# Dense matmuls of a two-block model on one core: operands at other word addresses within 256 words

## What is computed

```python
def hybrid_layer(x, ...):
    xn = rmsnorm(x, norm1_g)
    proj = xn @ w_in                       # split in eleven parts
    ...
    mixed = g_ssd * (y_ssd @ w_ssd_out) + g_mla * (y_mla @ w_mla_out) + g_gdn * (y_gdn @ w_gdn_out)
    h = x + mixed @ w_out
    f = jnp.square(jax.nn.relu(rmsnorm(h, norm2_g) @ w_up)) @ w_down
    return h + f

def swiglu(h, w_in, w_out):                # second model, widths 1024 -> 2 x 2816 -> 1024
    a, u = jnp.split(h @ w_in, 2, axis=-1)
    return (jax.nn.silu(a) * u) @ w_out
```

## Time and profile before

| | us |
|---|---|
| median of 3 runs (2468.61 to 2469.38) | 2469.3 |
| the profiled execution, whole | 2476.37 |
| its span (first to last instruction) | 2474.5 |
| TensorE busy | 2375.8 (96%) |
| weight loads busy | 2197.9 (89%) |
| VectorE busy | 1432.0 (58%) |
| ScalarE busy | 1246.8 (50%) |
| GpSimd busy | 301.3 (12%) |
| DMA moved | 380.98 MB, mean 154 GB/s |

### The profile page before, as it was taken

The page is one execution under the profiler, slowest core; times in us unless marked ns, Lnnn a source line. Parts: engine busy times, 40 slices in busy tenths (PEclk is TensorE's granted clock), DMA queues, the critical chain, the costliest instruction groups (busy, mean ns, idle before and its releaser), DMA issues.

```text
span 2474.5 us, 48016 instructions
## 1 busy us (share of the span) xinstructions
PE 2375.8 (96%) x21242; PEld 2197.9 (89%) x21242; DVE 1432.0 (58%) x2151; ACT 1246.8 (50%) x1846; POOL 301.3 (12%) x171
## 2 busy tenths in 40 slices
PE   6989999999999899899999999999999999998999
PEld 6979898999899798899999787887789998787999
DVE  6773875665467467756655247643335553676554
ACT  5745654554466475456544367542223453445543
POOL 5213000000141220001000004200000001331000
PEclk9999999999999999999999999999999999999999
DMA  5344354555444444445553336333325542223555
GB/s 195 127 155 169 137 179 151 198 184 190 164 170 149 153 160 147 173 142 204 189 186 122 119 107 219 119 119 137 119 85 188 205 155 88 81 93 137 176 190 181
DMA packets 55824, 380.98 MB, mean 154 GB/s; under 512 B 6081, under 2 KB 9665, under 8 KB 10305
## 3 DMA queue, kind: packets, MB, share of 16 engines
q1 hardware_dynamic: 54864, 374.59, 42.2%
q10 hardware_dynamic: 752, 3.33, 0.4%
HBM read 375.79 MB, written 1.05 MB: 152 GB/s over the span
## 4 chain that ended last, share of the span: by engine, by line
PE 75%; DVE 12%; ACT 7%; DMA 3%; issue 2%; POOL 0%; DVEq 0%; ACTq 0%; POOLq 0%
PE ps L950 20%; PE ps L951 19%; PE ps L952 19%; DVE r L2241 4%; ACT r L1577 2%; DMA ring<-in_win 2%; PE ps L1031 1%; PE ps L1032 1%; PE ps L1033 1%; PE ps L1079 1%; PE ps L909 1%; PE ps L871 1%; PE ps L988 1%; DVE slab L2330 1%; PE ps L989 1%
## 5 line engine op out<-in xcount | busy, mean ns | idle before, releaser
L950 PE MATMUL ps<-r,r 128*128 128x256 f32 (+1 forms) x4448 | 1321.0, 297 | 11.9 <-DVE r L2241 3.1
L951 PE MATMUL ps<-r,r 128*128 128x256 f32 (+1 forms) x4448 | 1306.5, 294 | 0.0
L952 PE MATMUL ps<-r,r 128*128 128x256 f32 (+1 forms) x4448 | 1305.9, 294 | 0.0
L2241 DVE TENSOR_TENSOR r<-ring,r 128x1024 fp32r<-128x1024 f32 x554 | 678.6, 1258 | 508.9 <-ACT r L1577 508.5
L950 PEld LDWEIGHTS ps<-r,r 128*128 128x128 f32 x4448 | 838.2, 188 | 49.5 <-issue 13.3
L952 PEld LDWEIGHTS ps<-r,r 128*128 128x128 f32 x4448 | 837.9, 188 | 24.9
L951 PEld LDWEIGHTS ps<-r,r 128*128 128x128 f32 x4448 | 838.3, 188 | 24.4 <-issue 0.5
L1577 ACT ACTIVATE r<-ring 128x1024 fp32r<-128x1024 f32 (+1 forms) x610 | 610.1, 1041 | 276.2 <-DMA ring<-in_fo 61.7
L3176 POOL TENSOR_TENSOR slab<-slab 128x512 f32<-128x512 f32 (+1 forms) x20 | 28.7, 1433 | 1234.4 <-ACT slab L1693 1214.1
L3128 POOL TENSOR_TENSOR r<-ring,r 128x1024 fp32r<-128x1024 f32 x56 | 132.7, 2393 | 226.1 <-ACT r L1577 216.2
L2330 DVE SCALAR_TENSOR_TENSOR slab<-ps,v,slab 128x255 f32<-128x255 f32 (+1 forms) x168 | 67.8, 475 | 76.0 <-ACT slab L1645 76.0
(11 more groups left out here) (348 smaller groups left out, 2522.5 us busy)
## 6 DMA issues: line engine op xcount, KB each, us to landing
ring<-in_win SPq DMA_DIRECT2D x74, 1024.0 KB, 4.8
ring<-in_ada SPq DMA_DIRECT2D x48, 1024.0 KB, 4.8
ring<-in_fi SPq DMA_DIRECT2D x44, 1024.0 KB, 4.8
ring<-in_fo SPq DMA_DIRECT2D x36, 1024.0 KB, 4.7
ring<-in_wup SPq DMA_DIRECT2D x32, 1024.0 KB, 4.7
ring<-in_wdn SPq DMA_DIRECT2D x32, 1024.0 KB, 4.7
ring<-in_hin SPq DMA_DIRECT2D x20, 1024.0 KB, 4.7
ring<-in_nqkv SPq DMA_DIRECT2D x12, 1024.0 KB, 4.8
```

What stands on the lines that cost most here:

```text
L950: self.mm(o, hi[:, k - k0, cs], xh, k == 0, False)
L951: self.mm(o, hi[:, k - k0, cs], xl, False, False)
L952: i = self.mm(o, lo[:, k - k0, cs], xh, False, k == last)
L2241: self.tt(K.low(p), K.raw(p), K.high(p).bitcast(F32), ALU.subtract).then_inc(*self.up("w_lo_v", p))
```

## The change

Only constants and offsets of the memory layout are changed. The slab is 96 words longer, so the ring and all that lies behind it move up by 96. xn starts at 224 (SHIFT), its low part at another 16 words on (OFF). `keep` is padded to 136 (KEEP) modulo 256. The low part of hid is 8 words further on. In block 2, 24 words of padding stand before h, 8 between its parts, and 248 behind it, so that everything from `early` on starts at 64. The view hg is given the same place as before, the first part of h, by a new name. `rounded` now makes its view from a multiple of 8 words below and cuts the front off. In the table, positions are words from the slab's start, modulo 256.

| operand | before | after |
|---|---|---|
| weight blocks (high, low, raw) | 96, 224 | 192, 64 |
| xn high, low | 40, 40 | 224, 240 |
| ys, ms, qn, kn | 40 | 136 |
| hid high, low | 40, 40 | 136, 144 |
| h high, low | 40, 40 | 64, 72 |
| hid2, read_of[0] | 40 | 64 |
| x2, constants | 96 | 192 |

The instructions of every engine, their order and their waits are the same ones in both kernels.

```diff
-ARENA = 34656
-SHIFT = 40
+ARENA = 34656 + 96
+SHIFT = 224
+KEEP = 136
+OFF = 16
...
     def rounded(self, at, n):
 
         self.names += 1
-        t = self.nc.alloc_sbuf_tensor_at(f"r{self.names}", [128, n], F32R, offset=self.home + 4 * at)
-        return t[:, 0:n]
-
-    def pair(self, A, kt, n):
+        more = at % 8
+        t = self.nc.alloc_sbuf_tensor_at(f"r{self.names}", [128, n + more], F32R, offset=self.home + 4 * (at - more))
+        return t[:, more:more + n]
+
+    def pair(self, A, kt, n, off=0):
         out = []
-        for _ in range(2):
+        for i in range(2):
+            A.at += i * off
             A(kt * n)
             out.append(blocks(self.rounded(A.at - kt * n, kt * n), kt))
         return out
...
-        self.xn = self.pair(A, 8, T)
+        self.xn = self.pair(A, 8, T, OFF)
...
-        A.at += (SHIFT - A.at) % 256
+        A.at += (KEEP - A.at) % 256
         keep = A.at
...
-        self.hid = self.pair(A, 32, T)
+        self.hid = self.pair(A, 32, T, 8)
...
         self.A1, self.A2, self.FA = A(8, 2), A(8, 2), A(8)
-        self.h = self.pair(A, 8, 512)
+        A.at += 24
+        first = A.at
+        self.h = self.pair(A, 8, 512, 8)
+        A.at += 248
         early = A.at
...
-        self.hg = blocks(self.slab[:, early - 8192:early - 4096], 8)[:, :, CTX]
+        self.hg = blocks(self.slab[:, first:first + 4096], 8)[:, :, CTX]
```

## The result

The changed kernel takes 2490.2 us (median of three runs, 2487.9 to 2492.7) where the kernel before takes 2469.3: the ratio is 1.0086, with a 95% interval of 1.0063 to 1.0109. It is slower by 21 us. The forecast, no change and 2469, was wrong; the time lies inside the range and within 2 us of rival 2's price, a nearness that is luck, as the part on the prediction shows.

What follows compares the result with a forecast made beforehand. TensorE was taken as the bound, with dense matmuls 79% of the 2474.5 us span. All terms were zero, so the sum was 0 us and the forecast the unchanged plain median, 2469 us; the range was 2418 to 2500.

Steps and rivals of the forecast that it cites:

- rival 2: Weight load and moving read meet, longest in h and hid2, little in xn: 20 us slower, 2489; chance 0.20.
- What bounds the kernel: TensorE, busy 2375.8 of 2474.5 us; dense matmuls take 1949 us, 79% of the span.
- These 24 cycles in 280: Dense 256-column matmuls: the only thing addresses could move on a large scale; at best 101 us gained.
- The loss goes with columns, not with loads: Dense matmuls: one load at either width, yet 512 columns lose 48 cycles against 24, so the load is not the cause.
- two distances, one rate: Wide rows stage at distance 56 starts every 232.5 ns, against 233 at distance 72, so the read's start does not matter.
- the check against a busy VectorE: Nine dense matmuls took 1.05 us both with VectorE idle and with it in the ring, so no other engine.
- rival 1: The moved dense stages: loss hangs on distance and new distances lessen it; half of 101 us gained, 2418; chance 0.32.
- zero change per matmul: Moved matmuls: the value chosen, bounded by 101 us gain and 40 us loss; no change has chance 0.38.
- The half-rate row: fp32 matmuls at two cycles a column start 216 ns apart at distance 72 and at 0: distance makes no difference.
- The row of 284 cycles: Narrow rows stage, moving read in two pieces: 118.3 ns a start, read as 2 cycles for each break in the stream.
- Other work: Weight split on VectorE and ScalarE, and DMAs: covered by idle time or unchanged, 0 us.
- Rival 3: Breaks alone between high and low parts of xn, hid and h: 5.9 us slower, 2475; chance 0.10.

Runs made afterwards that it cites:

- run 4: The probe: no model, TensorE alone running the three-matmul pattern over many distances, offsets and widths; 288 cycles at distance 0, 280 or 283 at 72.
- run 10: Changed kernel with every moving operand at distance 28 modulo 64, high and low parts alike: 2450.21 us, ratio 0.9903 to the kernel before.
- run 11: Changed kernel with high weights 32 words beyond low ones, moving operands at distance 48, no low-part offsets: 2444.62 us, ratio 0.9886 to the kernel before.
- run 1: Changed kernel with every operand pair back at its old distance, everything still 96 words further up: 2470.66 us, ratio 0.9998 to the kernel before.
- run 5: Changed kernel with high parts back at distance 72, low parts of xn, hid and h still offset: 2474.91 us, ratio 1.0012 to the kernel before.
- run 12: Changed kernel with high weights 32 words beyond low ones and moving operands at distance 4: 2462.15 us, ratio 0.9960 to the kernel before.

## Why the prediction was wrong, point by point

**What bounds the kernel**: right. 79% of the span is dense matmuls, and the whole loss is in them.

**The size of what addresses can move**: a number too big. "These 24 cycles in 280" are not all at stake. The lowest pitch that any of over 1000 combinations showed is 272 cycles at 256 columns and 544 at 512: at best 3.3 ns and 6.7 ns a matmul, 13344 x 3.33 + 1680 x 6.67 = 56 us, not 101. The Trainium skill, "TensorE: Matmul & The Clock Gate", section "Back-to-back issue gap", gives the rule that the prediction weighed, 109 and 216 ns, for a matmul on its own and not for a stream of loads and matmuls. No run here reaches it at either width; the nearest are 113.3 and 226.7 ns.

**"The loss goes with columns, not with loads"**: this is the step that failed. It was inferred from 280/256 and 560/512 being the same ratio, with one load of 128 columns each. The probe shows that the load does take part (288 against 272 cycles at distance 0 when the stationary operand shrinks from 128 to 64 columns; elsewhere a shorter load can be slower), and that the equal ratio is a property of a few distances such as 8 modulo 64: at distance 0 the pair is 288 and 544. A single ratio, taken at the only distance the trace had, was read as a law. The two other comparisons in support were of the same kind: the wide rows stage (distance 56) has the kernel's own distance with the sign turned, and the probe gives 560 cycles at 8 and at 56 alike but 544 at 0 and 549 at 16, so "two distances, one rate" was true of these two; and the check against a busy VectorE excluded an outside cause, but not an effect between TensorE's own two reads. The prediction itself said in rival 1 that equal rows at 72 and 56 prove little, and then gave the case that rests on them the highest chance. What the runs put in the place of "zero change per matmul": between -1.1 ns (wide h) and +3.3 ns (hid2) a moved matmul, 25.5 us in all, of which 4.2 come back as shorter waits.

**The half-rate row**: 216 ns at both distances was called the nearest row to distance 0. It was nearest by address and far by rate; at one column a cycle distance 0 costs 8 cycles that the half-rate stream does not show.

**The row of 284 cycles**: read as possible breaks in the stream. The probe gives 284 cycles at distance 56, the rows stages' distance, and a read in two pieces 280 at distance 72 and 284 at 56: the distance alone is enough for it, and pieces are not needed. In the kernel the rows stages went to 120.0 and 117.8 ns when their distance changed (runs 10 and 11). So that row was the one hint in the trace that distance matters, and it was given to another cause. One thing stays open: the change moved these stages too, to distance 0 for two matmuls of three and 56 for the third, and they stayed at 118.3 ns; the probe, which has 288 cycles for two pieces with all at 0, did not try this mixture.

**Other work at zero**: right. VectorE's split takes 1258 and 1254 ns, ScalarE's 1041 and 1040, and run 1 is even with the kernel before.

**Rival 1** was right that distance matters and wrong in the sign for these distances; that new ones can be better, runs 10 and 11 show (2450 and 2445 us, where it priced 2418 for half of its full gain).

**Rival 2** has the size: 20 us and 2489 forecast, 21 us and 2490 measured. That is luck: the price, 1.67 ns on all 12032, was taken from a row of another distance, the terms lie between -1.1 and +3.3 ns, their mean is 2.1 ns (25.5 us), and the waits that gave 4 us back were in no sum. Its place was half right. hid2 and the narrow h are at 120 as it said; but xn, "little", carries over half of the stages' 25.5 us, and the wide h, with distance 0 too, became shorter. That weight load and moving read act on each other is what the probe bears out. That it happens where "both now begin at the same place" is too simple: distance 24 is as bad as 0.

**Rival 3**: 5.9 us forecast, 2.2 measured in run 5, by 283 cycles in the narrow stages instead of the 281.3 implied, and the distance of the low parts accounts for it without any price for a break.

What the memory does inside to make some distances modulo 64 words worse isn't shown by any of these runs; they give the table, not the circuit, and since all blocks are multiples of 128 words long they can't say whether a matmul's read is held up by its own weight block or by the load of the next one. The Trainium skill, "SBUF — State Buffer", section "Who interferes with whom", says that "PE and ACT never wait on anyone". That no other engine slows TensorE agrees with the probe, where the others are idle and the pitches are the same. But TensorE's own two reads cost up to 27 cycles beyond 272 (299, the worst combination), so the sentence does not mean that the place of an operand is free.

## What to carry to other kernels

Where TensorE streams fp32r matmuls of 256 or 512 columns with a load of 128 before each, try the distance between the moving operand and the weight block, modulo 64 words; it costs nothing: 28 without offsets, or high weights 32 words further and distance 48, gave 1% here, and a badly chosen one loses as much. An inference about contention from rows that all sit at one distance isn't evidence; a probe with TensorE alone and one source line per distance gives the table in one run, though it can show one rhythm of two (run 12), so a candidate must be tried in the kernel itself. When the bound engine gets faster by 43 us, expect a part (12 us in run 11) to come back as waits between them.

## What the runs showed of the hardware that was not expected

- The pitch of a load-and-matmul pair has a period of 64 words in the distance of the two operands (a few of the probe's cases apart, see run 4), and all addresses 96 words further change nothing (ratio 0.9998).
- At 256 columns it takes 272, 277, 280, 283, 284, 285, 288, 291 up to 299 cycles; at 512, 544 to 568. With 64 to 224 moving columns it is 268 throughout, 128 columns at every distance: there a load-and-matmul pair has a floor of 112 ns that the moving columns don't set, so at 256 columns the best placement, 272, stands 4 cycles above it.
- Several rhythms exist for one set of addresses: 280 or 283 at distance 72, 281 or 288 at (0, +8), 283 or 291 at (32, +16), 544 or 568 at distance 60 and 512 columns, and in run 12 272 or 283. Once in one, a stage can stay in it for hundreds of matmuls or change in its middle: w_in of after repeats 118, 118, 117, 122, 120, 131 ns, w_up of layer 0 120, 117, 117 with the same operand, and w_up of layer 1 goes from 291 to 283 cycles at 1165 us.
- Widths disagree: without offsets distance 0 is, with 24, the worst at 256 columns (288) and the best at 512 (544).
